# A two-layer decoder in float32 on one core: mask added by TensorE, values with tokens on partitions, other portions of convolution taps, four more unsplit panels, other buffer addresses

## The chip, the cores and the metric

The kernel runs on one core of a Trainium2 chip. The metric is the device time of one execution in microseconds. TensorE (matrix products), VectorE (DVE), ScalarE (ACT), GpSimd (POOL) and SyncE (SP, which here only issues transfers) each work through a queue of their own in order, and wait for each other by semaphores.

## The reference

One sequence of T = 256 tokens, width D = 1024, two layers, all float32. A layer is a feed-forward half step, a token mixer and a second feed-forward half step:

```
h = rms_norm(x) * (1 + scale_i(c)) + shift_i(c)          # i = 0, 1, 2; scale, shift, gate from c
x = x + 0.5 * gate_0 * ((silu(h @ wg) * (h @ wu)) @ wd)  # 1024 -> 2816 -> 1024
z = h @ w_in                 # q, k, v of 12 heads of 64; u (2 x 1024); two gates (2 x 1024)
attention: 3 groups of 4 heads, dilation 1, 4, 16, windows 128, 512, 2048, causal;
           scores * 64**-0.5, masked with -1e30; the three groups of a head are merged by the
           softmax of their log denominators
conv:      u = a * sigmoid(g); 31 taps for each channel along the tokens, + bias;
           layer_norm; silu; @ conv_wo
x = x + gate_1 * ((sigmoid(g_a) * (o @ attn_wo) + sigmoid(g_c) * conv) @ w_out)
x = x + 0.5 * gate_2 * swiglu(h)
```

At the end comes a last RMS norm. Merging three groups by their log denominators is the same as one softmax over the keys of all three, and the kernel computes it so.

## The kernel before

**Panels.** All weights stream from memory once, in 200 panels of 128 partitions x 2048 float32 (1 MB), through a ring of six buffers (`raw`). A layer has 33 panels for the first feed-forward, 34 for the mixer and 33 for the second feed-forward. For a panel, float32 is either split or not. A split panel is rounded to the faster type float32r by ScalarE (`hi`, line 668, into `w_hi`), VectorE takes the rest (`lo`, lines 961 to 966, `w_lo` in place of the raw panel), and TensorE makes three products of 512 columns for each product of tiles: high with high, low with high, high with low (`three`, lines 319 to 322). The activations are split likewise (`hA_hi`, `hA_lo` for h; `mid_hi`, `mid_lo` for the hidden values; `hB` for y; `o` for the attention). An unsplit panel (`is_whole`, line 51: ten in each mixer) needs neither ScalarE nor VectorE: TensorE multiplies the float32 values directly, with `hF` (line 339). In these products the activation is the stationary operand and the weights move.

**Feed-forward.** `ffn(f)` (line 412) takes blocks of 256 hidden columns: gate and up panels for both token tiles, transposes of the product, down panel. At the very start of the kernel, the order is another: VectorE computes scales and shifts from c by 16 products of a row with chunks of `ada_w` (`ada_units`, line 1002; 512 KB for each chunk, ring of seven), eight of which give the first half of h's channels. The panels' first halves (b = 0) begin when that half is there.

**Mixer.** TensorE's order is written out by hand (`mix`, lines 451 to 649). Four blocks of u are projected; VectorE multiplies with the sigmoid (`gated`), TensorE transposes (`u_turn`), ScalarE copies to `conv_in` (channels on partitions). Three blocks of q and k follow, each rotated by VectorE (`rotate`) and transposed (`qk_turn`), then v. For each of four heads (three groups at once) come scores, mask and maximum, exponent, scaling by the reciprocal of the sum, transposes of the probabilities (`p_turn`), values (`pv`: output with 64 channels on partitions and tokens along them), with the six gate panels (`M_G` on) between these steps. Then come the product with the attention's output weights (`M_AO`), which VectorE multiplies with the sigmoids into `y` (line 1239), the transposes of the convolution's result (line 590), the last gate panels (`M_G3`), layer norm, convolution's output and `w_out`.

**Convolution.** It runs on VectorE: for each pair of channel blocks (128 channels each), 31 taps for each of the two blocks alternate, one instruction of 128x256 for a tap (lines 1146 and 1150), 248 in a layer. They are dealt out in portions between VectorE's other duties: `QUOTA` (line 47) by step of the projections, `HEAD_QUOTA` (line 48) three times for each head, and all that is left behind `y` (line 1240). TensorE's transposes of a pair wait for its last tap.

**SyncE** issues c, four chunks of `ada_w`, x, the parameters, the identity, three more chunks, panel 0, chunks to 9, panel 1, chunks to 16, then panels 2 to 5 (lines 271 to 292), and further panels as buffers come free.

Of the kernel before, what the change touches and what calls it, by code (L numbers as in the profile page):

```python
# [6 lines left out]
ALU = mybir.AluOpType  # L7
# [6 lines left out]
P = 128  # L14
# [30 lines left out]


QUOTA = (0, 0, 0, 2, 5, 9, 4, 9, 4, 9, 1, 9, 1, 9, 1, 7)
HEAD_QUOTA = (6, 6, 6)


def is_whole(p):
    return p % LAYER_PANELS - FFN_PANELS in WHOLE


def splits(p):

    l, i = divmod(p, LAYER_PANELS)
    return p - l * len(WHOLE) - sum(w < i - FFN_PANELS for w in WHOLE)


SPLIT_PANELS = [p for p in range(PANELS) if not is_whole(p)]
# [30 lines left out]
def ada_before(p):  # L92

    if p < 3:
        return (8, 10, 16)[max(p, 0)]
# [15 lines left out]
def decoder_program(nc, x_in, c_row, g_row, params, rope, ident, mask, ada_w, weights, out):  # L111
    with ExitStack() as ctx:
# [27 lines left out]
        hA_hi = sb("hA_hi", [P, KC, T], F32R)  # L140
        hA_lo = sb("hA_lo", [P, KC, T], F32R)
# [7 lines left out]
        mask_sb = sb("mask_sb", [P, TT, NG, T], BF16)  # L149
        rope_sb = sb("rope_sb", [P, 2, TT, HD])  # L150
        ident_sb = sb("ident_sb", [P, P])
        eps = sb("eps", [P, 1])
# [20 lines left out]
        att_at = room(16896)  # L173
        v_sb = at(att_at, "v_sb", [P, TT, NG * 256])
        probs = [at(att_at + 6144, "probs0", [P, NG, P]), at(att_at + 7680, "probs1", [P, NG, T])]
        probsT = at(att_at + 10752, "probsT", [P, NG, TT, T])
# [4 lines left out]
        gates_at = room(16384)  # L181
# [12 lines left out]
        glu_at = room(4096)  # L194
# [35 lines left out]
        score_done, masked_done, max_done, exp_done = sem("score_done"), sem("masked_done"), sem("max_done"), sem("exp_done")  # L230
        rden_done, prob_done, pT_done, probT_done = sem("rden_done"), sem("prob_done"), sem("pT_done"), sem("probT_done")
        pv_done, o_hi_done, o_lo_done = sem("pv_done"), sem("o_hi_done"), sem("o_lo_done")
# [32 lines left out]
        def _(sp):  # L265
# [28 lines left out]
            sp.dma_start(mask_sb[:], mask).then_inc(tables_in, 16)  # L294
# [21 lines left out]
        def _(pe):  # L316
# [95 lines left out]
            def ffn(f):  # L412
                n = ffn_norm(f)
                g = [gate_panels(f, j) for j in range(NJ)]
                if f == 0:
                    for b in range(2):
                        for j in range(2):
                            ready(g[j][b])
                            for tt in range(TT):
                                h_ready(0, tt, b)  # L420
# [6 lines left out]
                for j in range(2, NJ - 1):  # L427
                    both(g[j][0], hA, 0, gu(j))
# [22 lines left out]
            def mix(l):  # L451
# [37 lines left out]
                def scores(h):  # L489
                    if h == 0:  # L490
                        pe.wait_ge(qk_done, 2 * NG * (l + 1))
                    else:
                        pe.wait_ge(probT_done, 2 * (HPG * l + h))
                    for q in range(TT):
                        keys = (q + 1) * P
                        for g in range(NG):
                            part = slice((h % 2) * HD, (h % 2 + 1) * HD)
                            dst = S1[:, g, :] if q else S0[:, g, :]
                            mm = nc.tensor.matmul(dst, qkT[part, g, 0, h // 2, q * P:(q + 1) * P],  # L499
                                                  qkT[part, g, 1, h // 2, 0:keys], start=True, stop=True)  # L500
                        mm.then_inc(score_done, 1)

                def p_turn(h):
                    for q in range(TT):
                        pe.wait_ge(prob_done, 2 * (HPG * l + h) + q + 1)
# [6 lines left out]
                def pv(h):  # L512
# [3 lines left out]
                    if h == 2:  # L516
                        pe.wait_ge(o_lo_done, 2 * l + 1)
                    half, c = slice((h % 2) * HD, (h % 2 + 1) * HD), (h // 2) * T
                    for g in range(NG):
                        e = slice((HPG * g + h) * HD, (HPG * g + h + 1) * HD)  # L520
                        nc.tensor.matmul(ps[half, 3, c:c + T], v_sb[:, 0, e], probsT[:, g, 0, :],  # L521
# [909 lines left out]
```

## Time and profile before

| | us |
|---|---|
| median of 3 runs | 1407.45 (1404.75 to 1407.49) |
| profiled execution | 1404.21 |
| its span | 1402.4 |
| mean granted clock of TensorE | 0.956 of 2.4 GHz |

The span runs from the first to the last instruction of the profiled execution. A view names an instruction by its line and tiles; `x16` is how many records a row merges. A record's duration contains the pipeline's latency, so records of one engine overlap, and the pace of a row of like instructions is read from the starts. A product of unsplit float32 tiles shows as two records.

### The profile page before, as it was taken

To read this page: it belongs to the slowest core of one execution; us is meant where nothing else is said; L and a number is where in the kernel's file an instruction comes from. 1 tells how busy PE (TensorE), PEld (TensorE's weight loads), DVE (VectorE), ACT (ScalarE), POOL (GpSimd) and SP (SyncE) were. 2 spreads that over 40 slices of the span, in tenths; PEclk is the share of its full clock that TensorE was granted. 3 is DMA by queue.
4 is the path that set the end of the run, shared out by engine and by line. 5 is a ranking of instruction groups with operands and counts; after the bars stand their busy time and mean duration, and the time that the engine had idled before them with its cause. 6 is when DMAs were issued, how large, how long until landed. Compare 5 with 4: busy or idle time off the path is not lost.

```text
span 1402.4 us, 13828 instructions
## 1 busy us (share of the span) xinstructions
PE 1248.1 (89%) x5400; PEld 965.6 (69%) x5400; DVE 990.5 (71%) x1391; ACT 557.3 (40%) x580; POOL 2.2 (0%) x5
## 2 busy tenths in 40 slices
PE   1899999999952889999999999999998069999997
PEld 1688887667631678788878888776665057788885
DVE  5888886676789457778767888667677965654443
ACT  4443345232440445444355433442245043544431
POOL 0000000000000000000000000000000000000000
PEclk8999999999985999999999999999999589999999
DMA  9889983554320346899847888445432014355550
GB/s 372 346 308 371 376 322 120 210 194 146 112 74 0 120 150 244 346 342 350 321 153 285 338 342 336 163 168 195 150 121 100 21 60 165 139 206 180 184 207 30
DMA packets 52914, 293.41 MB, mean 209 GB/s; under 512 B 6640, under 2 KB 6896, under 8 KB 27120
## 3 DMA queue, kind: packets, MB, share of 16 engines
q1 hardware_dynamic: 51120, 289.35, 55.3%
q10 hardware_dynamic: 1728, 3.17, 0.6%
q8 instruction: 43, 0.70, 0.2%
q14 instruction: 23, 0.19, 0.0%
HBM read 291.42 MB, written 1.07 MB: 209 GB/s over the span
## 4 chain that ended last, share of the span: by engine, by line
PE 80%; DVE 13%; ACT 2%; DMA 2%; issue 1%; SPq 0%; DVEq 0%
PE ps L320 23%; PE ps L321 22%; PE ps L322 22%; PE ps L339 8%; DVE work L1150 8%; DMA raw<-in_weights 1%; DVE w_lo L959 1%; PE ps L499 1%; PE ps L387 1%; DMA x<-in_x_tok 1%; PE ps L521 1%; PE ps L371 1%; ACT L674 1%; DVE hF L1046 0%; ACT xn_h L681 0%
## 5 line engine op out<-in xcount | busy, mean ns | idle before, releaser
L320 PE MATMUL ps<-w_hi,hA_hi 128*128 128x512 f32 (+1 forms) x1024 | 412.8, 403 | 27.9 <-DVE hA_lo L959 27.9
L959 DVE TENSOR_TENSOR w_lo<-raw,w_hi 128x2048 fp32r<-128x2048 f32 x180 | 410.0, 2286 | 32.5 <-ACT w_hi L668 32.5
L668 ACT CAST w_hi<-raw 128x2048 fp32r<-128x2048 f32 x180 | 342.2, 1911 | 153.1 <-PE ps L322 90.3
L321 PE MATMUL ps<-w_lo,hA_hi 128*128 128x512 f32 (+1 forms) x1024 | 400.1, 391 | 0.0
L322 PE MATMUL ps<-w_hi,hA_lo 128*128 128x512 f32 (+1 forms) x1024 | 399.4, 390 | 0.0
L320 PEld LDWEIGHTS ps<-w_hi,hA_hi 128*128 128x128 f32 x1024 | 195.2, 191 | 73.8 <-issue 18.9
L321 PEld LDWEIGHTS ps<-w_lo,hA_hi 128*128 128x128 f32 x1024 | 195.5, 191 | 40.4 <-issue 3.3
L322 PEld LDWEIGHTS ps<-w_hi,hA_lo 128*128 128x128 f32 x1024 | 194.8, 190 | 41.1
L1150 DVE SCALAR_TENSOR_TENSOR work<-conv_in,par,work 128x256 f32<-128x256 f32 x480 | 193.7, 477 | 0.0
L974 DVE SCALAR_TENSOR_TENSOR product<-ada_raw,c_bc 128x1024 f32<-128x1024 f32 x144 | 171.0, 1220 | 2.3 <-DMA ada_raw<-in_ada_w 2.2
L339 PE MATMUL ps<-raw,hF 128*128 128x512 f32 x320 | 141.2, 594 | 0.0
L320 PE MATMUL ps<-w_hi,mid_hi 128*128 128x512 f32 x336 | 133.6, 398 | 2.3 <-DVE mid_lo L959 2.3
L322 PE MATMUL ps<-w_hi,mid_lo 128*128 128x512 f32 x336 | 133.1, 396 | 0.0
L321 PE MATMUL ps<-w_lo,mid_hi 128*128 128x512 f32 x336 | 133.0, 396 | 0.0
L959 DVE TENSOR_TENSOR mid_lo<-ps,mid_hi 128x512 fp32r<-128x512 f32 (+1 forms) x44 | 29.3, 667 | 117.1 <-ACT mid_hi L730 113.4
L339 PEld LDWEIGHTS ps<-raw,hF 128*128 128x128 f32 x320 | 59.4, 190 | 69.1 <-issue 69.0
L723 ACT ACTIVATE act<-ps 128x512 f32<-128x512 f32 (+1 forms) x48 | 27.1, 565 | 147.7 <-PE ps L322 147.7
L590 PE MATMUL ps<-ident_sb,work 128*128 128x128 f32 x32 | 6.5, 353 | 82.4 <-DVE work L1150 82.4
L730 ACT CAST mid_hi<-ps 128x512 fp32r<-128x512 f32 x40 | 23.5, 589 | 131.6 <-PE ps L387 131.6
L320 PEld LDWEIGHTS ps<-w_hi,mid_hi 128*128 128x128 f32 x336 | 63.2, 188 | 17.7 <-DVE mid_lo L959 2.9
L322 PEld LDWEIGHTS ps<-w_hi,mid_lo 128*128 128x128 f32 x336 | 63.2, 188 | 15.3
L321 PEld LDWEIGHTS ps<-w_lo,mid_hi 128*128 128x128 f32 x336 | 63.3, 188 | 15.0
(114 smaller groups left out, 791.4 us busy)
## 6 DMA issues: line engine op xcount, KB each, us to landing
raw<-in_weights SPq DMA_DIRECT2D x200, 1024.0 KB, 4.8
ada_raw<-in_ada_w SPq DMA_DIRECT2D x144, 512.0 KB, 6.8
gate_bc<-gate_scratch ACTq DMA_DIRECT2D x6, 512.0 KB, 6.8
x<-in_x_tok SPq DMA_DIRECT2D x1, 1024.0 KB, 9.5
out_tok<-xn_h SPq DMA_DIRECT2D x4, 256.0 KB, 2.2
c_bc<-in_c_row SPq DMA_DIRECT2D x1, 512.0 KB, 4.4
c_bc<-in_g_row SPq DMA_DIRECT2D x1, 512.0 KB, 6.5
mask_sb<-in_mask SPq DMA_DIRECT2D x1, 384.0 KB, 16.4
```

Of the source, the lines that this page charges most:

```text
L320: nc.tensor.matmul(out_ap, stat[0], mov[0], start=start, stop=False)
L321: nc.tensor.matmul(out_ap, stat[0], mov[1], start=False, stop=False)
L322: return nc.tensor.matmul(out_ap, stat[1], mov[0], start=False, stop=stop)
L339: mm = nc.tensor.matmul(out_ap, hF[:, k, t], raw[:, p % RAW, c], start=(k == 0), stop=(k == KC - 1))
L371: mm = nc.tensor.transpose(ps[:, 2 * b + tt, i * P:(i + 1) * P], xn_of(n)[:, tt, k * P:(k + 1) * P], ident_sb[:])
L387: mm = nc.tensor.transpose(ps[:, bank, c:c + P], mid[:, tt, kk * P:(kk + 1) * P], ident_sb[:])
L668: nc.scalar.copy(w_hi[:, s % HI, :], raw[:, p % RAW, :]).then_inc(hi_done, 1)
L723: nc.scalar.activation(act[:, tts[0]:tts[-1] + 1, :], ps[:, bank + tts[0]:bank + tts[-1] + 1, 0:256], ACT.Silu).then_inc(silu_done, 1)
L730: nc.scalar.copy(mid_hi[:], cols(bank)).then_inc(mid_hi_done, 1)
L959: return nc.vector.tensor_tensor(dst, whole, hi_part.bitcast(F32), ALU.subtract)
L974: nc.vector.scalar_tensor_tensor(out=product[:, q % 2, :], in0=ada_raw[:, q % ADA_RING, :], scalar=1.0, in1=c_bc[:], op0=ALU.mult, op1=ALU ...
L1150: nc.vector.scalar_tensor_tensor(out=work[:, c, :], in0=conv_in[:, c, t:t + T], scalar=par[:, o:o + 1], in1=work[:, c, :], op0=ALU.mult, o ...
```

## The change

- The mask is no longer added by VectorE. TensorE writes it into the score banks first, as a product of a 16-bit identity with the 16-bit mask, and adds the scores to it; ScalarE's copy of q is scaled by 64 ** -0.5. VectorE takes the maximum, and ScalarE the exponent, from the bank directly.
- The probabilities are not scaled. In `pv` they are the stationary operand and v moves, so that o has tokens on partitions; for all heads VectorE multiplies o once with the reciprocals, and TensorE transposes it (`o_turn`).
- ScalarE computes tap 0 of each channel block with the bias behind its copy to `conv_in`. VectorE's 240 other taps have larger portions, and 10 taps stand between the low part of o and y.
- Gate panels are taken in halves (one token tile each), in another order between the attention's steps; the transposes of the convolution's first two pairs stand among them, ahead of the output product.
- The first four panels of the kernel are unsplit; the start's transfers and VectorE's chunks are in another order, and h's low parts come later.
- `hA` and the tiles in the three shared regions start at 64, 192, 128 and 256 bytes modulo 512 from the block's start (before: 0, 96, 96, 96).

```diff
+FIRST_WHOLE = 4
-QUOTA = (0, 0, 0, 2, 5, 9, 4, 9, 4, 9, 1, 9, 1, 9, 1, 7)
-HEAD_QUOTA = (6, 6, 6)
+QUOTA = (0, 0, 0, 0, 12, 11, 11, 11, 11, 11, 4, 11, 4, 11, 4, 16)
+HEAD_QUOTA = ((8, 8, 4), (8, 8, 4), (6, 6, 2), (6, 6, 4))
 def is_whole(p):
-    return p % LAYER_PANELS - FFN_PANELS in WHOLE
+    return p < FIRST_WHOLE or p % LAYER_PANELS - FFN_PANELS in WHOLE
...
-        def room(nbytes):
+        def room(nbytes, phase=None):
             o = top[0]
-            top[0] += (nbytes + 31) // 32 * 32
+            if phase is not None:
+                o += (base + phase - o) % 512
+            top[0] = o + (nbytes + 31) // 32 * 32
             return o
...
+        hA_at = room(2 * KC * T * 4, 64)
-        att_at = room(16896)
+        att_at = room(16896, 192)
-        gates_at = room(16384)
+        gates_at = room(16384, 128)
-        glu_at = room(4096)
+        glu_at = room(4096, 256)
...
-            load_ada(4)
+            load_ada(1)
             sp.dma_start(x[:], x_in).then_inc(x_load, 16)
+            sp.dma_start(ident_sb[:], ident).then_inc(consts_in, 16)
             sp.dma_start(par[:], params).then_inc(consts_in, 16)
-            sp.dma_start(ident_sb[:], ident).then_inc(consts_in, 16)
-            load_ada(7)
+            load_ada(8)
             load(0)
-            load_ada(9)
             load(1)
             load_ada(16)
...
                 def scores(h):
+                    nc.tensor.matmul(S0, ident16, mask_sb[:, 0, :, 0:P], start=True, stop=False, skip_group_check=True)
+                    nc.tensor.matmul(S1[:, 0:2, :], ident16, mask_sb[:, 1, 0:2, :], start=True, stop=False,
+                                     skip_group_check=True)
+                    nc.tensor.matmul(S1[:, 2, :], ident16, mask_sb[:, 1, 2, :], start=True, stop=False,
+                                     skip_group_check=True)
...
                 def pv(h):
+                    for q in range(TT):
+                        terms = [(g, k) for g in range(NG) for k in range(q + 1)]
+                        for i, (g, k) in enumerate(terms):
+                            e = slice((HPG * g + h) * HD, (HPG * g + h + 1) * HD)
+                            mm = nc.tensor.matmul(ps[:, 3, q * 256 + h * HD:q * 256 + (h + 1) * HD],
+                                                  probsT[:, g, k, q * P:(q + 1) * P], v_sb[:, k, e], start=(i == 0),
+                                                  stop=(i == len(terms) - 1), skip_group_check=True)
+                    mm.then_inc(pv_done, 1)
+
+                def o_turn():
+                    pe.wait_ge(o_done, l + 1)
+                    for c in range(2):
+                        for tt in range(TT):
+                            mm = nc.tensor.transpose(ps[:, 3, c * T + tt * P:c * T + (tt + 1) * P],
+                                                     o_sb[:, tt, c * P:(c + 1) * P], ident_sb[:])
+                    mm.then_inc(oT_done, 1)
+
+                def g_half(i, tt):
+                    group(M_G + i, i % 2, (6, 4, 6)[i // 2], (tt,))
+
+                def conv_turn(pr):
+                    pe.wait_ge(conv_step, (KC * l + 2 * pr + 2) * (TAPS - 1))
...
                 scores(0)
                 ready(base + M_V1)
                 v1(0)
                 v1(1)
                 pe.wait_ge(v_done, 2 * l + 1)
                 p_turn(0)
+                g_half(0, 0)
                 pv(0)
                 scores(1)
+                g_half(0, 1)
+                g_half(1, 0)
                 p_turn(1)
+                g_half(1, 1)
                 pv(1)
                 scores(2)
+                g_half(2, 0)
+                g_half(2, 1)
                 p_turn(2)
+                g_half(3, 0)
                 pv(2)
                 scores(3)
+                g_half(3, 1)
+                pe.wait_ge(raw_gate_done, 3 * l + 1)
+                g_half(4, 0)
                 p_turn(3)
+                g_half(4, 1)
                 pv(3)
+                pe.wait_ge(raw_gate_done, 3 * l + 2)
+                conv_turn(0)
+                g_half(5, 0)
+                o_turn()
+                conv_turn(1)
+                g_half(5, 1)
...
+                conv_turn(2)
+                conv_turn(3)
...
+                    for c in (2 * i, 2 * i + 1):
+                        o, b = C_LAYER * l + C_CW + c * TAPS, C_LAYER * l + C_CB + c
+                        nc.scalar.activation(work[:, c, :], conv_in[:, c, 0:T], ACT.Identity, bias=par[:, b:b + 1],
+                                             scale=par[:, o:o + 1]).then_inc(conv_first, 1)
...
                 for h in range(HPG):
-                    masked(h)
+                    maxima(h)
+                    conv(HEAD_QUOTA[h][0])
                     lo(base + 19 + 2 * h)
-                    conv(HEAD_QUOTA[0])
-                    row_scales(h)
-                    conv(HEAD_QUOTA[1])
+                    conv(HEAD_QUOTA[h][1])
+                    if h == 3:
+                        o_scale()
                     lo(base + 20 + 2 * h)
-                    conv(HEAD_QUOTA[2])
-                    if h == 2:
-                        head_out(0)
-                head_out(1)
+                    conv(HEAD_QUOTA[h][2])
+                o_low()
+                conv(10)
                 dve.wait_ge(sig_gate_done, 2 * l + 1)
...
+            dve.wait_ge(c_ready, 1)
+            ada_units(0, 1)
             for tt in range(TT):
                 norm_scale(0, tt)
-            ada_units(0, 8)
+            ada_units(1, 8)
             finish_norm(0, 0, 7)
-            ada_units(8, 10)
-            lo(0)
-            norm_lo(0, 0, 0)
-            norm_lo(0, 1, 0)
-            lo(1)
-            ada_units(10, 16)
+            ada_units(8, 16)
             finish_norm(0, 1, 15)
             norm_full(0, 0)
             norm_full(0, 1)
-            lo(2)
-            norm_lo(0, 0, 1)
-            norm_lo(0, 1, 1)
+            for b in range(2):
+                for tt in range(TT):
+                    norm_lo(0, tt, b)
```

## Rows read from the trace of the kernel before

**Rows 1.** The page: busy time of each engine, and the chain by engine.
```profile
PE 1248.1 (89%) x5400; PEld 965.6 (69%) x5400; DVE 990.5 (71%) x1391; ACT 557.3 (40%) x580; POOL 2.2 (0%) x5
...
PE 80%; DVE 13%; ACT 2%; DMA 2%; issue 1%; SPq 0%; DVEq 0%
```

**Rows 2.** Waits, whole span: who waited for whom, us in total, times, longest.
```profile
PE ps L590 <- DVE work L1150: 82.4, 4, 23.3
```

**Rows 3.** The chain in order of time, 332 to 475: start, length, what.
```profile
407.17 17.41 DVE work L1150 x44
...
425.23 23.76 DVE work L1150 x60
```

**Rows 4.** Stretches of the first layer: each engine's busy time, TensorE's clock, DMA.
```profile
259.00:407.00 148.00, 144.93 (x588) 94.75 (x587) 107.43 (x198) 56.26 (x67) 0.00 (x0) 1.00 0.39 139
407.00:449.00 42.00, 1.12 (x4) 0.72 (x4) 42.00 (x108) 1.54 (x3) 0.00 (x0) 0.55 0.06 24
```

**Rows 5.** Groups by line and shape, whole span: busy, mean ns | idle before.
```profile
L974 DVE SCALAR_TENSOR_TENSOR product<-ada_raw,c_bc 128x1024 f32<-128x1024 f32 x144 | 171.0, 1220 | 2.3 <-DMA ada_raw<-in_ada_w 2.2
...
L693 ACT ACTIVATE hF<-ps,modb,gs 128x128 f32<-128x128 f32 x48 | 18.1, 457 | 22.4 <-PE ps L371 22.4
...
L1188 DVE SCALAR_TENSOR_TENSOR probs<-ps,mask_sb 128x768 f32<-128x768 f32 x8 | 7.7, 958 | 5.9 <-PE ps L499 5.9
```

**Rows 6.** VectorE's timeline, first layer: start, length, instruction [idle before].
```profile
292.82 1.22 DVE L1176 TENSOR_TENSOR rope_a<-ps,rope_sb 128x1024 f32<-128x1024 f32 x1 [4.12 <-PE ps L339]
```

**Rows 7.** The chain again: an unsplit panel, transposes, values, scores.
```profile
260.32 6.87 PE ps L339 x16
...
343.31 0.98 PE ps L509 x9
...
347.03 0.58 PE ps L521 x2
...
349.12 2.16 PE ps L499 x12
```

**Rows 8.** TensorE's timeline: first and last of rows of like products.
```profile
216.27 0.39 PE L320 MATMUL ps<-w_hi,mid_hi 128*128 128x512 f32 x1
...
219.08 0.40 PE L320 MATMUL ps<-w_hi,hA_hi 128*128 128x512 f32 x1
...
399.98 0.47 PE L320 MATMUL ps<-w_hi,o_hi 128*128 128x512 f32 x1 [1.01 <-DVE o_lo L959]
...
478.56 0.39 PE L320 MATMUL ps<-w_hi,hA_hi 128*128 128x512 f32 x1
...
494.65 0.39 PE L322 MATMUL ps<-w_hi,hA_lo 128*128 128x512 f32 x1
...
498.32 0.40 PE L322 MATMUL ps<-w_hi,hB_lo 128*128 128x512 f32 x1
...
503.24 0.39 PE L322 MATMUL ps<-w_hi,hB_lo 128*128 128x512 f32 x1
```

**Rows 9.** ScalarE's timeline: the sigmoid of the gates.
```profile
400.69 2.77 ACT L901 ACTIVATE gates<-gates 128x3072 f32<-128x3072 f32 x1
```

**Rows 10.** Timeline of the start: TensorE's three beginnings, ScalarE's split of panel 2.
```profile
31.80 0.77 PE L320 MATMUL ps<-w_hi,hA_hi 128*128 128x512 f32 x1 [12.93 <-DVE hA_lo L959]
...
37.76 1.92 ACT L668 CAST w_hi<-raw 128x2048 fp32r<-128x2048 f32 x1 [3.90 <-DMA raw<-in_weights]
...
48.17 0.47 PE L320 MATMUL ps<-w_hi,hA_hi 128*128 128x512 f32 x1 [3.29 <-DVE hA_lo L959]
...
62.91 0.50 PE L320 MATMUL ps<-w_hi,mid_hi 128*128 128x512 f32 x1 [1.57 <-DVE mid_lo L959]
```

**Rows 11.** The chain of the start.
```profile
3.33 9.53 DMA x<-in_x_tok
```

**Rows 12.** Stretches of the start and first feed-forward, columns as rows 4.
```profile
60.00:75.00 15.00, 13.43 (x63) 10.80 (x63) 10.49 (x10) 8.69 (x7) 0.00 (x0) 1.00 0.51 187
165.00:180.00 15.00, 15.00 (x69) 12.29 (x68) 12.96 (x16) 6.82 (x5) 0.00 (x0) 1.00 0.99 385
```

More of the change, by code:

```diff
@@ L515, in pv @@
                         pe.wait_ge(v_done, 2 * (l + 1))
-                    if h == 2:
[L517 to L521, printed above, removed]
-                                         start=(g == 0), stop=False, skip_group_check=True)
-                        mm = nc.tensor.matmul(ps[half, 3, c + P:c + T], v_sb[:, 1, e], probsT[:, g, 1, P:T],
-                                              start=False, stop=(g == NG - 1), skip_group_check=True)
@@ new lines, in conv_turn @@
+                def conv_turn(pr):
+                    pe.wait_ge(conv_step, (KC * l + 2 * pr + 2) * (TAPS - 1))
+                    for c in range(2):
+                        for tt in range(TT):
+                            k = 2 * pr + c
+                            mm = nc.tensor.transpose(ps[:, 4 + 2 * (k // 4) + tt, (k % 4) * P:(k % 4 + 1) * P],
+                                                     work[:, k, tt * P:(tt + 1) * P], ident_sb[:])
+                    mm.then_inc(cT_done, 1)
@@ L1133, in mix @@
                 base, n, end = mix_base(l), 3 * l + 1, mix_base(l) + MIX_PANELS
-                taps_total = KC * TAPS
+                steps = KC * (TAPS - 1)
                 done = 0
@@ L1182, in rotate @@
                     nc.vector.tensor_tensor(roped[:], rope_a[:], rope_b[:], ALU.add).then_inc(rope_done, 1)
-                def masked(h):
-                    for q in range(TT):
-                        u = 2 * HPG * l + 2 * h + q
-                        dve.wait_ge(score_done, u + 1)
-                        nc.vector.scalar_tensor_tensor(out=probs[q][:], in0=(S1 if q else S0), scalar=HD ** -0.5,
-                                                       in1=mask_sb[:, q, :, 0:(q + 1) * P], op0=ALU.mult,
-                                                       op1=ALU.add).then_inc(masked_done, 1)
-                    for q in range(TT):
-                        u = 2 * HPG * l + 2 * h + q
-                        dve.wait_ge(masked_done, u + 1)
-                        nc.vector.tensor_reduce(negmax[:, 2 * h + q:2 * h + q + 1], probs[q][:], AX.XY, ALU.max,
-                                                negate=True).then_inc(max_done, 1)
@@ L1239, in mix @@
                         nc.vector.tensor_tensor(y[:, tt, c], acc(half, tt), gates[:, tt, c], ALU.mult).then_inc(ya_done, 1)
[L1240 removed]
+                conv(steps)
                 for hf in range(2):
@@ L1319, in _ @@
             norm_full(0, 1)
-            lo(2)
-            norm_lo(0, 0, 1)
-            norm_lo(0, 1, 1)
+            for b in range(2):
+                for tt in range(TT):
+                    norm_lo(0, tt, b)
             for l in range(DEPTH):
@@ L1420 @@
         "g_row": a["final_g"].reshape(1, D), "params": params, "rope": rope, "ident": np.eye(P, dtype=np.float32),
-        "mask": mask.astype(ml_dtypes.bfloat16), "ada_w": ada_w, "weights": weights,
+        "mask": np.concatenate([mask.reshape(P, -1), np.eye(P, dtype=np.float32)], axis=1).astype(ml_dtypes.bfloat16), "ada_w": ada_w, "weights": weights,
     }
```

147 lines of the change are left out of this document (65 added, 82 removed).

## The prediction

> **What bounds the kernel now.** First the page's busy shares and its chain [rows 1]: TensorE is busy 89% of the span and makes 80% of the chain that ended last, VectorE 13%, DMA 2%. So time goes only where TensorE gets less work, or waits less. The waits name the one large hole: the transposes of the convolution (line 590) wait 82.4 us for the taps of line 1150, in four waits of which the longest is 23.3 [rows 2], two in each layer. The chain puts this in the first layer behind the product with the attention's output weights: 17.41 us of 44 taps from 407.17, then 23.76 us of 60 taps from 425.23 [rows 3]; one tap is 23.76 / 60 = 0.396 us. The stretches say why [rows 4]: from 259 to 407 VectorE is busy only 107.4 of 148 us, and from 407 to 449 it alone works, at a granted clock of 0.55 for TensorE (the lower level, 1.2 GHz, for most of it). The second layer repeats it. The profiled execution took 1404.21 us for a span of 1402.4; the median of the runs is 1407.45, 3.2 above. I sum against the profiled one and add the difference to the median.
>
> **Larger portions of taps, tap 0 on ScalarE.** Before, the portions are 70 taps in the projections and 4 x 18 in the heads, 142 of 248; 106 are left behind y (106 x 0.396 = 42.0; the rows' 41.8 go from 407.17 to 449.0). After, VectorE has 240; 117 in the projections, 70 in the heads and 10 behind the low part of o make 197; 43 are left, 43 x 0.396 = 17.0 us. If y ends at the same time, the last transposes come 41.8 - 17.0 = 24.8 us earlier. Whether y does is a matter of two questions.
>
> Does VectorE fit 55 more steps between 259 and 407? It loses the masked scores (eight shorter ones and eight like that of 958 ns [rows 5]; in a layer about 4 x (0.48 + 0.88) = 5.4 us), 16 small reciprocals become two (1 us in a layer) and 6 of the eight first taps (2 us), and gains 61 taps (24.2) and a scaling of o (0.7): 107.4 + 24.9 - 8.4 = 123.9 of 148. It fits on average; what matters is each portion, since the engine takes its queue in order. In the projections two panels take TensorE 5.44 + 6.87 + 0.44 to 0.87, some 13 us; VectorE has in them a rotation 3.6 or a gating 0.6, one low part 2.2, and 15 or 22 taps (5.9 or 8.7): 11.7 or 11.5. The tightest places: the third gating would be done at 271.0, where its transposes are due at 272.1, behind panel 6; the first rotation at 293.4 instead of 292.82 [rows 6], done at 297.0, its transposes due behind panel 10 at 297.6; the portion of 16 taps ends at 333.0, and the first scores now come at 333.6. In the heads the portions are 20, 20, 14 and 16 taps with one or two low parts, against some 15 us between scores: VectorE idles 2 us before each maximum. So no portion costs TensorE anything, with 0.6 to 1.1 us in hand at the tightest, and 2 to 3 us for each gating or rotation that is late by a further portion of 11 (4.4 us); that is a rival. The first taps on ScalarE: two more instructions of about 0.46 each behind each copy (I read 457 ns from the scaling of 128x128 [rows 5]; twice that width costs no more than double), where ScalarE is idle more than half of 259 to 407 [rows 4]; cost 0. Uncovered it would be 1 us for each of four.
>
> **Attention.** TensorE's own work up to y: scores take 2.16 us for a head (349.12) [rows 7]. The mask adds three products of 384, 512 and 256 columns at 16 bits. By the spacing 0.2267 us for 512 columns [rows 8] that is 0.51, with a change of stationary 0.6; bounds 0.3 and 0.9. Eight heads in the two layers: 4.8. The values with tokens on partitions: six products of 256 and 128 columns (2.09 from 347.03 to 349.12 [rows 7]) become nine of 64 columns with another stationary tile of 128x128 for each, 18 records. The nearest rows with a new stationary tile and few columns are the nine transposes in 0.98, 0.109 each [rows 7]: 18 x 0.109 = 1.96, no change. Bounds: half of it by the columns alone (0.054 each, 1.0), and up to 0.24 each, 4.3, if the loads aren't hidden: -9 to +18 us over eight heads. I take 0. Four transposes for o add 0.44 in each layer, four early transposes of the convolution go to where TensorE works anyway. I laid the new order out from 332.4 with these durations: p of the four heads turned at 341, 356, 371 and 386, the maximum and exponent of each 3 to 6 us earlier; pv(3) done at 391.5, o scaled at 392.5, turned at 395.9 and split at 397.4, before the attention's output product, which can start at 399.8 (now 399.98 [rows 8]): masks and turns are paid by the waits for scaled probabilities and for o's low part that are gone. The change adds one wait on VectorE: the scaling of o waits for the values of all heads, from 385.7 to 391.7, and behind it queue the low part of panel 26, 4 taps, o's low part and 10 taps; of these only o's low part is due soon (397.4 for 399.8), panel 26 is used after 425. On ScalarE the copy of o waits for its turn with the third gates' copy behind it, which is due only at 400. ScalarE's copy of the third gates follows at 400, then the sigmoid of 2.77 [rows 9] with its table, done at 405.0; y ends at 407.6 against 407.2. So 0.4 of the 24.8 is lost: 24.4 for each layer, 48.8 together. The clock falls in the wait of 17 us as it does now in two of 18 and 23, so nothing more comes back there.
>
> **First four panels unsplit, start reordered.** A split panel of the gates takes TensorE 24 x 0.2267 = 5.44 us, an unsplit one 6.87 (16 records) [rows 7]: on TensorE alone 4 x 1.43 = 5.7 us worse. But the start isn't bound there. Now TensorE starts at 31.80, stops, starts the second halves at 48.17 and the first down product at 62.91 [rows 10]; x lands at 12.86 [rows 11]. Up to x 3.67 MB are asked for, so landing is about 3.0 us + MB / 0.38 per us; that gives panel 2 (13.55 MB) at 38.7 where ScalarE takes it at 37.76 [rows 10]. In the new order x is behind 2.1 MB: 8.5. The first chunk of the conditioning product is done before it, the normalised rows at 12.3, seven more chunks at 1.15 each (page 1.22 with its overlap [rows 5]) by 20.5, the first scales at 20.9, ScalarE's half of h at 22.5; panel 0 lands at 22.1. TensorE starts at 22.6, about 4 us of it at 1.2 GHz (as 31.8 to 35.8 now), and ends two panels at 38.3. The last chunk lands at 35.9, is multiplied at 37.1; the scales and VectorE's half of h are done at 38.9: 0.6 of wait. Two panels to 52.8. Down panel 4 lands at 44.1, is split by 51.1; the second hidden product and its low part are done at 55.2. The first down product starts at 55.3 instead of 62.91: 7.6 us. Bounds: 0 (if the low parts of h, now behind panel 4's, come last) and 10 (if no chunk is waited for and the low parts follow 2 us sooner). Is it given back in the same feed-forward? DMA moves 385 GB/s at a share of 0.99 there, but only 187 at 0.51 from 60 to 75 [rows 12], when the rings are full: 7 us of room, and each panel lands 10 us or more ahead of its use. I keep it.
>
> **Operands at other addresses.** Counted from the start of the block, the tiles of h before lie at 0 modulo 512 bytes, those of mid, y, o at 96. Matmuls of one form differ by just this: 71 steps from 478.56 to 494.65 with hA give 0.2266, 21 from 498.32 to 503.24 with hB 0.2343, 12 from 216.27 to 219.08 with mid 0.2342 [rows 8]. After, these tiles lie at 64, 192, 128, 256, all multiples of 64. If 96, the only one that isn't, is what costs 7.6 ns, then (1008 + 192 + 48 + 48) = 1296 matmuls give 9.8 us. Bounds: 0; the far ends are rivals. I take 9.8.
>
> The Trainium skill ("SBUF — State Buffer", the cachelines in its section on the DMA port swizzle) has lines of 16 bytes and prices only the crossing of them; 0 and 96 are alike by it, and the term would be 0, the sum 1350. The trace has two spacings, so I don't follow it.
>
> **Sum.** 48.8 + 7.6 + 9.8 = 66.2 (masks and turns are inside the 0.4 us by which y ends later). 1404.2 - 66.2 = 1338.0; at the median 1341.
>
> **Rivals.**
> A. The addresses give nothing: the 96 is chance, and y's and mid's products are slow for another reason. For it: all slow tiles also lie high in the buffer. 1341 + 10 = 1351.
> B. The granule is 128 bytes or more: h at 64 then joins the slow. 3072 x 7.6 ns = 23.3 lost, hB and mid at best 7.7 won: 1351 + 16 = 1367. No row has a stationary tile at 64.
> C. The new addresses free all matmuls. An unsplit product's record takes 6.87 / 16 = 0.4294, twice 0.2147; if that is two passes of 512 columns, a split one could do 0.2147: 3072 x 12 ns + 1296 x 19.6 ns = 62, in place of 9.8: 1289. Half of it, 1315. Against: nothing but the 96 is seen to matter. The Trainium skill ("TensorE: Matmul & The Clock Gate", Back-to-back issue gap) gives 512 / 2.4 + 2.5 = 216 ns for such a matmul; an estimate by it is 57 us in place of 9.8. The trace doesn't reach it in any split product.
> D. Loads of the 18 stationary tiles aren't hidden: +18, and the output product later by as much: 1359. The transposes' 0.109 speaks against.
> E. The other side: VectorE's portions come late. Each gating, rotation and maximum behind a portion (nine a layer, 18 in all) holds TensorE by the portion's 4.4 us: 79 - 66 = 13 slower, 1420. It decides from a mean lateness of 66 / 18 = 3.7 us. Against: the layout has none late by more than its slack, since the rows show 3 to 5 us of idleness before each such step [rows 6].
>
> **Chances.** Forecast 0.60, A 0.13, B 0.06, C 0.12, D 0.05, E 0.04. The range takes in A, D and the half of C, and the bounds of start, mask and values: 1316 to 1362. No change is told apart from about 0.2%, 2.8 us. Faster 0.95, same 0.01, slower 0.04 (E).
>
> **What would show it.** One wait for taps in each layer, of about 17 us instead of 18 + 23, and 43 taps behind y; y ends 407 - 8 of start - 2 of addresses, near 397 in the first layer; the transposes of the gatings and rotations without a wait for VectorE; first down product at 55; spacings 0.2267 in mid's and hB's products; a head's values near 2 us. Wrong would be waits of TensorE on lines of gating, rotation or maximum (E), a spacing of hA other than 0.2267 (B, C), or a feed-forward 0 that ends less than 7 us earlier.

## The result, and the profile after

The median went from 1406.1 us (1404.56 to 1407.49) to 1366.99 us (1366.07 to 1369.2, four runs): ratio 0.9724, 95% interval 0.9706 to 0.9742. That is 39 us faster where the prediction said 66, and 5 us above the upper end of its range. The span of the profiled execution fell by 37.1 us, from 1402.4 to 1365.3.

First the page of the changed kernel: TensorE's busy share and its share of the chain that ended last, to be held against [rows 1].

```profile
span 1365.3 us, 13844 instructions
...
PE 1270.0 (93%) x5440; PEld 967.8 (71%) x5448; DVE 966.4 (71%) x1341; ACT 545.7 (40%) x574; POOL 2.2 (0%) x5
...
PE 86%; DVE 6%; ACT 3%; DMA 3%; issue 2%; SPq 0%; DVEq 0%; ACTq 0%
```

VectorE's share of the chain has more than halved, from 13% to 6%. TensorE's waits (who waited for whom, us in total, times, longest) say where from, and show another line that grew:

```profile
PE ps L558 <- DVE work L1179: 37.6, 2, 18.8
...
PE ps L537 <- ACT probsT L872: 2.9, 3, 1.4
```

The wait for the taps, 82.4 us in four before [rows 2], is 37.6 in two. The product of values and probabilities (line 537) waits for ScalarE's copy of the turned probabilities, 1.3 and 1.4 us ahead of the last head's values. The kernel before has such a wait too, 0.9 us in each layer:

```profile
PE ps L521 <- ACT probsT L840: 1.8, 2, 0.9
```

There the values stood right behind the transposes, so TensorE had nothing to do while ScalarE copied. Here half a gates panel stands between, and the copy is late for another reason. The chain of the changed kernel through the end of the first attention stage (start, length, what) shows both, and answers to [rows 3]:

```profile
370.66 1.96 PE ps L537 x18
...
378.92 4.83 DMA raw<-in_weights
...
383.77 0.02 ACT w_hi L705
383.80 1.78 issue
385.58 0.47 ACT probsT L870
386.05 0.71 ACT probsT L872
...
386.81 2.22 PE ps L537 x18
...
402.39 2.48 DVE y L1266 x4
404.87 17.03 DVE work L1179 x43
...
421.95 1.12 PE ps L558 x4
```

One block of 43 taps in 17.03 us stands where 44 and 60 stood. Its two stretches, the columns as in [rows 4]:

```profile
254.00:405.00 151.00, 147.57 (x627) 98.50 (x629) 124.18 (x238) 52.46 (x63) 0.00 (x0) 1.00 0.39 138
405.00:422.00 17.00, 0.05 (x1) 0.06 (x1) 17.00 (x44) 2.42 (x3) 0.00 (x0) 0.54 0.10 43
```

VectorE is busy 124.2 us of 151 ahead of y, against 107.4 of 148 in [rows 4] and 123.9 of 148 forecast. In the wait TensorE's granted clock is 0.54, for most of it the lower of its two levels, 1.2 GHz.

The start, to be held against [rows 10] and [rows 11]: TensorE's first product of a panel, its first down product, and, in the second fence, the transfer of x.

```profile
23.24 1.19 PE L348 MATMUL ps<-raw,hF 128*128 128x512 f32 x1 [8.13 <-ACT hF L730]
...
55.09 0.50 PE L329 MATMUL ps<-w_hi,mid_hi 128*128 128x512 f32 x1 [1.57 <-DVE mid_lo L990]
```
```profile
1.65 7.46 DMA x<-in_x_tok
```

And the spacing of like products, to be held against [rows 8]: 87 steps with hA from the first to the second of these rows, 23 with mid, 58 with hB.

```profile
447.37 0.40 PE L331 MATMUL ps<-w_hi,hA_lo 128*128 128x512 f32 x1
...
467.66 0.40 PE L331 MATMUL ps<-w_hi,hA_lo 128*128 128x512 f32 x1
...
72.41 0.39 PE L329 MATMUL ps<-w_hi,mid_hi 128*128 128x512 f32 x1
...
77.75 0.39 PE L331 MATMUL ps<-w_hi,mid_lo 128*128 128x512 f32 x1
...
479.13 0.39 PE L330 MATMUL ps<-w_lo,hB_hi 128*128 128x512 f32 x1
...
492.41 0.40 PE L331 MATMUL ps<-w_hi,hB_lo 128*128 128x512 f32 x1
```

hA takes (467.66 - 447.37) / 87 = 0.2332 us a step where [rows 8] gave 0.2266; mid takes 0.2322 instead of 0.2342; hB 0.2290 instead of 0.2343. So the tile with the most products got slower, and the two that were to become fast improved by 2.0 and 5.3 ns instead of 7.6.

Set against each other at points of the work, the changed kernel leads by 7.8 us at the first down product (55.09 for 62.91), 5.9 at the end of the first feed-forward, 4.8 at the first scores, 2.3 at the end of the first y (404.87 for 407.17), 27.1 at the transposes of the convolution behind it (421.95 for 449.03). From there to the end of the second y (1069.95 for 1085.84) the lead falls to 15.9; it is 40.7 behind the second block of taps, 37.1 at the end. Everything that was forecast to be won at the start and behind y is there; it leaks away between, and 3.6 us more behind the second block of taps.

### The profile page after: what moved, and what is told of

It reads as the page before. It is cut to its first block, busy times and chain, and to the rows that moved or that the text cites. A ratio compares the mean times of both kernels' runs of the same rounds, so it can differ in the third digit from the quotient of the medians.

```text
span 1365.3 us, 13844 instructions
## 1 busy us (share of the span) xinstructions
PE 1270.0 (93%) x5440; PEld 967.8 (71%) x5448; DVE 966.4 (71%) x1341; ACT 545.7 (40%) x574; POOL 2.2 (0%) x5
## 4 chain that ended last, share of the span: by engine, by line
PE 86%; DVE 6%; ACT 3%; DMA 3%; issue 2%; SPq 0%; DVEq 0%; ACTq 0%
PE ps L329 23%; PE ps L330 23%; PE ps L331 23%; PE ps L348 12%; DVE work L1179 2%; DMA raw<-in_weights 2%; PE ps L537 1%; PE ps L515 1%; PE ps L396 1%; PE ps L380 1%; ACT L711 1%; DMA x<-in_x_tok 1%; ACT xn_h L718 0%; ACT gates L932 0%; PE ps L485 0%
## 5 line engine op out<-in xcount | busy, mean ns | idle before, releaser
L990 DVE TENSOR_TENSOR w_lo<-raw,w_hi 128x2048 fp32r<-128x2048 f32 x176 | 401.0, 2287 | 34.9 <-ACT w_hi L705 34.4
L329 PE MATMUL ps<-w_hi,hA_hi 128*128 128x512 f32 (+1 forms) x992 | 402.7, 406 | 11.7 <-DVE hA_lo L990 11.7
L705 ACT CAST w_hi<-raw 128x2048 fp32r<-128x2048 f32 x176 | 334.3, 1909 | 174.0 <-PE ps L331 92.9
L330 PE MATMUL ps<-w_lo,hA_hi 128*128 128x512 f32 (+1 forms) x992 | 391.4, 395 | 0.0
L331 PE MATMUL ps<-w_hi,hA_lo 128*128 128x512 f32 (+1 forms) x992 | 390.8, 394 | 0.0
L329 PEld LDWEIGHTS ps<-w_hi,hA_hi 128*128 128x128 f32 x992 | 188.4, 190 | 60.0 <-issue 19.7
L330 PEld LDWEIGHTS ps<-w_lo,hA_hi 128*128 128x128 f32 x992 | 188.5, 190 | 43.2 <-issue 2.9
L348 PE MATMUL ps<-raw,hF 128*128 128x512 f32 x384 | 172.2, 601 | 8.1 <-ACT hF L730 8.1
L348 PEld LDWEIGHTS ps<-raw,hF 128*128 128x128 f32 x384 | 72.3, 193 | 90.1 <-issue 89.7
L1093 DVE TENSOR_TENSOR mid<-act,ps 128x512 f32<-128x512 f32 (+1 forms) x48 | 30.9, 643 | 49.0 <-ACT act L760 48.9
```

Of the source, the lines that this page charges most:

```text
L329: nc.tensor.matmul(out_ap, stat[0], mov[0], start=start, stop=False)
L330: nc.tensor.matmul(out_ap, stat[0], mov[1], start=False, stop=False)
L331: return nc.tensor.matmul(out_ap, stat[1], mov[0], start=False, stop=stop)
L348: mm = nc.tensor.matmul(out_ap, hF[:, k, t], raw[:, p % RAW, c], start=(k == 0), stop=(k == KC - 1))
L705: nc.scalar.copy(w_hi[:, s % HI, :], raw[:, p % RAW, :]).then_inc(hi_done, 1)
L990: return nc.vector.tensor_tensor(dst, whole, hi_part.bitcast(F32), ALU.subtract)
```

## The experiments

Theory: three terms stand (start, taps, masks with values), the address term has the wrong sign, and something in the attention stage makes the turned probabilities late. Each experiment takes out or puts in one of these. All times are medians, ratios against the kernel before on the same chip.

**The old addresses in the changed kernel.** All else stays.

```diff
-        hA_at = room(2 * KC * T * 4, 64)
+        hA_at = room(2 * KC * T * 4)
-        att_at = room(16896, 192)
+        att_at = room(16896, 96)
-        gates_at = room(16384, 128)
+        gates_at = room(16384, 96)
-        glu_at = room(4096, 256)
+        glu_at = room(4096, 96)
```

> The changed kernel with the tiles back at 0, 96, 96, 96 modulo 512 (only the 16-bit identity behind the mask still shifts small tiles). Theory 1 (where the stationary tile starts sets the pace): the steps of hA fall from 0.2333 to 0.2280 us (2976 x 5.3 ns = 15.8 less), those of mid, hB, o and end rise by 2 to 4 ns (1296: 3 more); 1367 - 13 = 1354. Theory 2 (the pace of hA fell because of what the other engines do beside it in the new order, not by its address): hA stays at 0.2333 and the time at 1367.

1354.39 us (1352.58 to 1357.7), ratio 0.9633 (0.9617 to 0.9648). Over all consecutive products (rows 0.20 to 0.26 us apart) hA is back at 0.2278 from 0.2334, mid and hB at 0.234. So the new addresses cost the changed kernel 12.6 us instead of bringing 9.8.

**hA alone back at 0**, the others at the new addresses (the first pair of lines above).

> The changed kernel with hA alone back at 0 modulo 512, the other tiles at their new addresses. Theory 1: hA at 0.2280 or faster, mid and hB unchanged at 0.232 and 0.230, so 1367 - 16 = 1351, 3 better than with all at the old addresses. Theory 2: 1367.

1353.1 us (1350.64 to 1353.98), ratio 0.9618 (0.9604 to 0.9633): 13.9 us are hA's. By the steps it should be 2976 x 5.3 ns = 15.8; where the other 2 us are was not followed. Its trace also settles where the lead goes in the first feed-forward: the lead of 7.7 us at the first down product (55.20) is still 8.0 at the last product of the first feed-forward (221.76 for 229.81), where the changed kernel has 5.9 (223.86). The loss in the first feed-forward is hA's.

**The new addresses in the kernel before**, nothing else (the function `room` with its phase, and 64, 192, 128, 256 in the four places).

> The kernel before with the new addresses 64, 192, 128, 256 and nothing else of the change. Theory 1: hA from 0.2280 to 0.2333 (+16), the others -3: 1406 + 13 = 1419. Theory 2: 1406. As I forecast it: 1396.

1416.76 us (1416.38 to 1417.97), ratio 1.0076 (1.0059 to 1.0093): slower by 10.7 us by the ratio. The sign does not depend on the rest of the change.

**The products by themselves.** This kernel leaves the whole computation out: TensorE alone issues 96 split products for each of twelve addresses of the stationary tile with the moving one at 0, then five pairs of addresses, then unsplit products.

```python
for p in PHASES:                  # 0 32 64 96 128 160 192 224 256 320 384 448
    run(s[p], w[0], 8)
for a, b in MOVING:               # (0, 64) (64, 64) (96, 96) (96, 0) (0, 96)
    run(s[a], w[b], 8)
```

> Leaves out the whole computation: TensorE alone runs split-type products of 512 columns (96 in a row for each case, a new stationary tile for each, in the order of a split panel) with the stationary tile at 0, 32, 64, 96, 128, 160, 192, 224, 256, 320, 384 and 448 modulo 512, moving tile at 0; then moving tiles at 64 and 96; then unsplit products at 0 and 96. Theory 1: the same steps without company, 0.227 at 0, 0.233 at 64, 0.234 at 96, and a pattern between. Theory 2: one pace for all. Theory 3 (it is the distance of stationary and moving tile that counts): stationary 64 with moving 64 and 96 with 96 are as fast as 0 with 0. With the rival C of the forecast some address gives 0.2147.

TensorE's timeline of that kernel: the first rows of ten of the seventeen blocks. The last letter is the address modulo 512 of the stationary tile (statA) or the moving one (movA): A to H are 0 to 224 in steps of 32, I, K, M, O are 256, 320, 384, 448. A block's step is the distance to the first row of the next block over 96. The first block (both at 0) began with steps of 427 ns, so its value is that of its last 55 steps.

```profile
79.27 0.40 PE L79 MATMUL ps<-movA,statC 128*128 128x512 f32 x1
...
101.67 0.39 PE L79 MATMUL ps<-movA,statD 128*128 128x512 f32 x1
...
124.14 0.39 PE L79 MATMUL ps<-movA,statE 128*128 128x512 f32 x1
...
213.23 0.39 PE L79 MATMUL ps<-movA,statI 128*128 128x512 f32 x1
...
234.99 0.40 PE L79 MATMUL ps<-movA,statK 128*128 128x512 f32 x1
...
301.68 0.39 PE L79 MATMUL ps<-movC,statA 128*128 128x512 f32 x1
...
323.67 0.40 PE L79 MATMUL ps<-movC,statC 128*128 128x512 f32 x1
...
345.46 0.39 PE L79 MATMUL ps<-movD,statD 128*128 128x512 f32 x1
...
367.24 0.40 PE L79 MATMUL ps<-movA,statD 128*128 128x512 f32 x1
...
389.72 0.40 PE L79 MATMUL ps<-movD,statA 128*128 128x512 f32 x1
```

| stationary tile at | 0 | 32 | 64 | 96 | 128 | 160 | 192 | 224 | 256 |
|---|---|---|---|---|---|---|---|---|---|
| step in ns, moving at 0 | 226.7 | 233.3 | 233.4 | 234.4 | 232.3 | 233.3 | 228.9 | 233.3 | 226.7 |

The blocks follow each other without a gap, so the rows give (101.67 - 79.27) / 96 = 233 ns at 64, (124.14 - 101.67) / 96 = 234 at 96, (234.99 - 213.23) / 96 = 227 at 256. 320, 384 and 448 repeat 64, 128 and 192 (233.3, 232.4, 229.0). The kernel's tiles agree: hA at 64 had 233.2, mid at 128 232.2, hB at 192 229.0. And the pairs: with both at 64 the step is (345.46 - 323.67) / 96 = 227, with both at 96 (367.24 - 345.46) / 96 = 227 again; stationary 0 and moving 64 gives 229, which is the value of 192; stationary 0 and moving 96 gives 233, the value of 160. For all the addresses tried, what decides is the difference between the two, stationary less moving, modulo 256, and only 0 is the fast case. In the kernels the moving tiles lie at 0, so there the stationary tile's own address decides. No case is faster than 226.7. The unsplit products' records take 0.429 us at 0, 32 of them in 13.73, as those of the gates panels.

**All four tiles at 0.**

```diff
-        hA_at = room(2 * KC * T * 4, 64)
+        hA_at = room(2 * KC * T * 4, 0)
```
and likewise 192, 128 and 256 become 0.

> The changed kernel with h and all three shared regions at 0 modulo 256, as the weights are. If the distance between stationary and moving tile modulo 256 sets the pace, every split product steps by 0.2267 to 0.228: hA as with h alone at 0 (1353), and the 1296 others from 0.232 to 0.2267, 6 less: 1347. If only h's tile had mattered: 1353. If absolute addresses count, the others stay at 0.232: 1353.

1344.96 us (1341.9 to 1350.14), ratio 0.9566 (0.9539 to 0.9592). 22 us less than the changed kernel from one number in four places, though the four runs spread over 8 us. A stretch of hA from the timeline, 81 steps of 0.2270:

```profile
443.37 0.39 PE L331 MATMUL ps<-w_hi,hA_lo 128*128 128x512 f32 x1
...
461.76 0.39 PE L331 MATMUL ps<-w_hi,hA_lo 128*128 128x512 f32 x1
```

**The same, with ScalarE's splits behind the turned probabilities.** In the changed kernel the gates' panels are halved around the heads. In ScalarE's timeline (start, length, instruction, idle before) its split of panel 26 stands ahead of the last head's turned probabilities, and waits for a transfer:

```profile
383.77 1.91 ACT L705 CAST w_hi<-raw 128x2048 fp32r<-128x2048 f32 x1 [3.83 <-DMA raw<-in_weights]
385.58 0.47 ACT L870 COPY probsT<-ps 128x384 f32<-128x384 f32 x1
```

That transfer starts at 378.92, when TensorE ends the second half of a gates panel at 378.91 and with it frees the buffer. In the kernel before, this gates panel was taken whole and ended at 376.2, the transfer was there at 380.9, and the split stood ahead of the last head's exponents, so it was over long before that head's probabilities were turned. The edit puts two splits of each layer behind those copies:

```diff
                 exps(1)
-                hi(base + 23)
                 turned(1)
+                hi(base + 23)
...
-                hi(base + 26)
                 turned(3)
+                hi(base + 26)
```

> As e5, and ScalarE's rounding of panels 23 and 26 of the mixer stands behind its copies of the turned probabilities of heads 1 and 3, not ahead. If the wait for these panels' transfers (4.8 us each behind the release of panels 17 and 20, with 1.3 and 1.4 us of TensorE's waits before the values of head 3 and a stretch at half clock in the second layer) is what makes the attention longer than laid out, 1.5 to 2 us less in each layer: 1344. If it is the mask products alone, no change: 1347.

1341.05 us (1340.76 to 1341.13), ratio 0.9534 (0.952 to 0.9548): 3.9 us less by the medians. That size is uncertain: the two ratios' intervals just overlap, and the profiled executions are only 1.1 us apart. The traces show the effect itself more plainly. From the first scores to the end of y this version takes 74.6 us in the first layer and 74.7 in the second, the one without the edit 76.6 and 76.8: 1.9 and 2.1 us less, and TensorE's waits for the turned probabilities are gone from the list. Behind y part is given back in the profiled execution: the granted clock from 460 to 480 is 0.91 there and 1.00 without the edit; why was not followed. The same place in its ScalarE timeline: the copies go first, and the panel's split no longer waits to speak of.

```profile
376.27 0.48 ACT L870 COPY probsT<-ps 128x384 f32<-128x384 f32 x1 [2.11 <-PE ps L526]
...
377.85 1.91 ACT L705 CAST w_hi<-raw 128x2048 fp32r<-128x2048 f32 x1 [0.18 <-DMA raw<-in_weights]
```

**The old portions of taps in the changed kernel.**

```diff
-QUOTA = (0, 0, 0, 0, 12, 11, 11, 11, 11, 11, 4, 11, 4, 11, 4, 16)
-HEAD_QUOTA = ((8, 8, 4), (8, 8, 4), (6, 6, 2), (6, 6, 4))
+QUOTA = (0, 0, 0, 2, 5, 9, 4, 9, 4, 9, 1, 9, 1, 9, 1, 7)
+HEAD_QUOTA = ((6, 6, 6), (6, 6, 6), (6, 6, 6), (6, 6, 6))
-                conv(10)
```

> The changed kernel with the portions of taps of before and no 10 taps behind the low part of o. 142 of 240 taps are then dealt out, 98 are left behind y, 55 more than now: 55 x 0.396 = 21.8 us in each layer, so 1367 + 43 = 1410 if the larger portions cost TensorE nothing where they stand. If they make gatings, rotations or maxima late (rival E), part of it comes back: below 1400.

1410.4 us (1409.17 to 1413.11), ratio 1.0025 (1.0015 to 1.0036). 43.4 us slower than the changed kernel, for 2 x 55 taps x 0.396 = 43.6: each tap moved ahead of y is worth its full length, and without this part the change as made is slightly slower than the kernel before.

**The old start in the changed kernel**: no unsplit first panels (`FIRST_WHOLE = 0`), the old order of the first loads, of the normalisation and of the conditioning product.

> The changed kernel with the start of before: four split panels, old order of transfers, chunks and low parts. If the 7.8 us that the first down product is earlier last to the end, 1367 + 7.8 = 1375. If the full DMA of the first feed-forward eats them, 1367 to 1370.

1373.7 us (1369.81 to 1375.99), ratio 0.9763 (0.9745 to 0.9782): the start is worth 6.7 us by the medians, 5.5 by the ratios, with intervals that leave some 2 to 9. Its first down product is at 62.37.

```profile
62.37 0.50 PE L330 MATMUL ps<-w_hi,mid_hi 128*128 128x512 f32 x1 [1.57 <-DVE mid_lo L996]
```

**More taps ahead of y**, on top of the version with all tiles at 0 and the splits later. VectorE waited 12.6 us in two layers for the values before it scaled o, and 22.5 before the maxima; 36 more taps go there, and 7 are left behind y.

```diff
-HEAD_QUOTA = ((8, 8, 4), (8, 8, 4), (6, 6, 2), (6, 6, 4))
+HEAD_QUOTA = ((8, 8, 4), (8, 8, 10), (6, 6, 6), (6, 23, 4))
-                conv(10)
+                conv(19)
```

> The kernel is e6 (all four operands at 0 modulo 256, panels' splits behind the turned probabilities) with 36 more taps per layer put into portions ahead of y, so that 7 taps in place of 43 stand behind it. Theory (a tap moved ahead of y saves its price on VectorE behind y, 0.396 us, as long as VectorE had idle time where it is put): 36 x 0.396 = 14.3 us per layer, 28.5 in all, so 1341 - 28 = about 1312. Rival (VectorE's idle time ahead of y is used up: it idled 6.3 us ahead of o's scaling and 3.7 us ahead of y's sum in the kernel after, 3.4 and 2.6 ahead of the maxima, so 14 us of taps overfill it): o's scaling or y come later by up to 5 us in each layer, 1317 to 1325, and a wait of TensorE or ScalarE on VectorE shows within the attention stage.

1312.29 us (1310.83 to 1312.6), ratio 0.9331 (0.9315 to 0.9347): 28.8 less than without, 54.7 less than the changed kernel. Its wait for taps and the chain of its first layer, then y in the version without these taps:

```profile
PE ps L558 <- DVE work L1179: 9.1, 2, 4.6
```
```profile
395.99 2.48 DVE y L1266 x4
398.48 2.78 DVE work L1179 x7
401.30 1.12 PE ps L558 x4
```
```profile
394.89 2.48 DVE y L1266 x4
```

The stretch 340 to 396 has VectorE busy 38.6 us without these taps and 52.2 with them, and TensorE busy 55.65 and 56.00 of 56: first without, then with.

```profile
340.00:396.00 56.00, 55.65 (x258) 38.65 (x256) 38.55 (x74) 22.52 (x26) 0.00 (x0) 1.00 0.33 113
```
```profile
340.00:396.00 56.00, 56.00 (x258) 38.91 (x257) 52.23 (x109) 21.84 (x28) 0.00 (x0) 1.00 0.32 113
```

y comes 1.1 us later in the first layer (395.99 for 394.89), but that lag was there ahead of the added taps: the first scores' records start at 323.84 for 322.74. From them to the end of y it is 74.6 us in both versions, and in the second layer 74.7 in both. So nothing of the rival shows.

**All four tiles at 0 in the kernel before**, nothing else: the forecast's address term alone, at the addresses that the rule names (`room` with its phase, and 0 in the four places).

> The kernel before with nothing changed but the addresses: all four operands of the split products (hA, mid, hB, o's) at 0 modulo 256. This is the forecast's address term alone, with the addresses that the difference rule names. Theory (the step of a product follows from the difference of the stationary and the moving address modulo 256): mid, hB and o go from 0.234 to 0.227 or 0.228 us, hA stays at 0.228, so the forecast's 9.8 us are there and more: about 1395 (1392 to 1398). Rival (the steps within the kernel are set by something else, such as the moment at which the stationary tile is written): within 3 us of the kernel before, 1403 to 1409.

1397.44 us (1395.64 to 1397.95), ratio 0.9937 (0.9923 to 0.9952): 8.9 us faster by the ratio, 7 to 11 by its interval. A stretch of mid, 23 steps of 0.2265:

```profile
79.83 0.39 PE L324 MATMUL ps<-w_hi,mid_hi 128*128 128x512 f32 x1
...
85.04 0.39 PE L326 MATMUL ps<-w_hi,mid_lo 128*128 128x512 f32 x1
```

## Why the prediction was wrong, by its steps

**The step that failed is "Operands at other addresses".** It read two spacings in the trace, 0.2266 for tiles at 0 and about 0.2343 for tiles at 96, and that reading was right: the products alone give 226.7 and 234.4 ns at these addresses. It then chose the explanation "96 is the only one that isn't a multiple of 64", which readings at two addresses could not tell from "everything but 0". The runs show the second: 64, 128 and 192 all miss the fast case, by 6.7, 5.6 and 2.2 ns. So instead of 1296 products gaining 7.6 ns, 2976 lost 5.3 (15.8 us) and the others gained 1 to 6 ns (about 3 us). Forecast -9.8, measured +12.6 by taking the addresses back: a miss of 22.4 us. The size would have been right at the right addresses: the last experiment measures -8.9 for it.

**Rival B had the sign and the victim** (h at 64 joins the slow), and came to 1367. The measured 1366.99 agrees, but not wholly for its reasons: it gave hB and mid up to 7.7 us of gain where they have about 3, its 23.3 us for hA (for 3072 products; the changed kernel has 2976) were 13.9 by the runs and 15.8 by the steps, and it knew nothing of the late probabilities. It had 0.06, because I had asked which rule fits the two addresses best, not how many rules fit them; 1367 lay outside the range for the same reason. A (nothing) and C (all faster) are both refuted. On C the Trainium skill ("TensorE: Matmul & The Clock Gate", Back-to-back issue gap) gives 216 ns as the gap of an isolated product of 512 columns; the same section puts a stream of loads and products at about 131 ns each. With TensorE alone at work, the best of seventeen blocks was 226.7, above both, so none of the addresses tried frees that time. The "SBUF — State Buffer" page of the Trainium skill, with its lines of 16 bytes, does not tell these addresses apart either, while the runs do, over 256 bytes.

**A second step failed in the attention: "pv(3) done at 391.5" left out what the moved gates halves do to a buffer.** The layout counts from first scores at 332.4; in the changed kernel they begin with the mask's product at 327.61, 4.8 earlier. "p of the four heads turned at 341, 356, 371 and 386" came true within 0.4 us: the transposes begin at 336.1, 351.0, 366.1 and here

```profile
381.53 1.15 PE L526 MATMUL ps<-ident_sb,probs 128*128 128x128 f32 x9
```

The values of the last head end at 389.0 instead of 391.5 - 4.8 = 386.7, and y at 404.87 instead of 402.8. The forecast followed ScalarE's queue with the transfers taken as landed. The panel's second half now ends 2.7 us later than the whole panel did (7.5 later counted from the first scores), the transfer into its buffer starts at 378.92 and takes 4.83, and the split that waits for it stands ahead of a copy that TensorE wants. With the splits behind the copies and all tiles at 0, y ends 75.2 us behind the mask's first product, which is the forecast's 407.6 - 332.4. The step cost 1.9 and 2.1 us up to y in the two layers by the traces, 3.9 by the medians. In the second layer TensorE's clock falls after its wait: the granted clock is 0.96 from 1046 to 1052 and 0.76 from 1052 to 1058, and the 18 records of values that take 1.96 us at 370.66 take 2.96:

```profile
1050.24 2.96 PE ps L537 x18
```
```profile
1046.00:1052.00 6.00, 4.60 (x27) 3.72 (x25) 0.00 (x0) 2.98 (x3) 0.00 (x0) 0.96 0.41 142
1052.00:1058.00 6.00, 6.00 (x20) 3.76 (x20) 4.47 (x6) 0.00 (x0) 0.00 (x0) 0.76 0.15 63
```

The two together are 26.3 us, and the prediction missed by 26.0. The version with both taken out measured 1341.05 against the predicted 1341. That this meets so closely is in part luck: the profiled executions are 63.4 us apart where 66.2 was forecast, the start brought less than its 7.6, and the second step's size is uncertain by more than a microsecond.

**The taps were right.** 43 behind y in 17.03 us (17.0 forecast), one wait a layer of 18.8, clock 0.54 in it. The 55 that moved are worth 43.4 us in both layers by their own experiment. The fit of VectorE (123.9 of 148 forecast, 124.2 of 151 measured) held, and no gating, rotation or maximum made TensorE wait: rival E is refuted. In the first layer the lead grows by 24.8 across the block of taps, the number forecast before the 0.4 for y.

**The start was right in its points and nearly in its worth.** TensorE starts at 23.24 (22.6 forecast), the first down product at 55.09 (55.3). 7.6 was forecast, 7.8 stands in the trace at that point, 6.7 in the medians and 5.5 in the ratios. The 1.9 us lost by the end of the first feed-forward are hA's: with hA alone back at 0 they are not lost.

**Masks and values were right in size.** The mask's products and the scores behind them (the mask's second product, of 512 columns, has no record here):

```profile
327.61 0.33 PE L506 MATMUL ps<-mask_all 128*128 128x384 bf16 x1
327.98 0.27 PE L509 MATMUL ps<-mask_all 128*128 128x256 bf16 x1
328.19 1.15 PE L515 MATMUL ps<-qkT 64*128 64x128 f32 x7
```

328.19 - 327.61 = 0.58 us a head, 0.6 forecast. The values' 18 records take 1.96 us, which is the forecast number, and rival D's 18 us are refuted. It is 0.109 us a record, as for the transposes and twice the 0.054 of the columns alone, so something other than the columns sets it; whether that is the load of the stationary tile was not tested. That ScalarE's first taps and the late scaling of o cost nothing follows from the waits, where neither appears; neither was undone alone. In the fastest version 7 taps a layer are still behind y.

## What to carry to other kernels

When two groups of instructions differ and one property separates them, count the rules that fit before you extrapolate to a value that no row shows, and give the move away from the known good value its full price times the number of instructions behind it; the tile with most products was the one moved off it. Here the better edit was to copy the good value, not to choose new ones. When a piece of work is moved later, ask which buffer it frees, which transfer waits for that buffer, and which instruction stands behind the transfer's user in its engine's queue. And where an engine's portions are hidden and show idle time, go on filling until the idle time before the next dependent step is nearly used up: the last 36 taps a layer were still worth their full length.

## What the runs showed of the hardware

The step of a split product of 128 x 128 with 512 columns, each with a new stationary tile, depends on where the stationary and the moving operand lie relative to one another: 226.7 ns when their addresses are equal modulo 256 bytes, 228.9 at a difference of 192, 232.3 at 128, 233.3 at 32, 64, 160 and 224, 234.4 at 96. It was measured for this form of product alone, in steps of 32 bytes, with the moving operand at 0, 64 and 96; what in the memory or in the engine makes it so stays open. In this kernel the fast case at all tiles is worth 22 us, 1.6%, against the addresses that were chosen.
